# Sixteen experts on one core: the next expert's up product is issued ahead of this one's down product, into a second accumulator bank

## The reference, cut to what matters

```python
def _moe(h, w_router, b_router, w1, w3, w2):
    ...
    out = jnp.zeros_like(h)
    for e in range(N_EXPERTS):
        he = jax.nn.silu(h @ w1[e]) * (h @ w3[e])
        out = out + gates[:, e:e + 1] * (he @ w2[e])
    return out
```

## Time and profile before

| what | value |
|---|---|
| median of 3 runs | 994.59 us (994.1 to 994.79) |
| profiled execution, its own time | 996.42 us |
| profiled execution, span of the core's instructions | 994.6 us |
| PE busy | 936.2 us, 94% of the span |
| DMA | 230.74 MB, mean 232 GB/s |
| granted TensorE clock, mean | 0.986 of full |
| `up(1)` starts / `down(15)` ends | 322.9 us / 598.9 us |

### The profile page before, as it was taken

The page is one execution under the profiler, slowest core; times in us unless marked ns, Lnnn a source line. Parts: engine busy times, 40 slices in busy tenths (PEclk is TensorE's granted clock), DMA queues, the critical chain, the costliest instruction groups (busy, mean ns, idle before and its releaser), DMA issues.

```text
span 994.6 us, 11764 instructions
## 1 busy us (share of the span) xinstructions
PE 936.2 (94%) x4268; PEld 513.5 (52%) x4269; DVE 416.4 (42%) x894; ACT 304.7 (31%) x693; POOL 31.4 (3%) x54
## 2 busy tenths in 40 slices
PE   3999999999998999987999999999989999999998
PEld 1464456565443344332455445455765546577763
DVE  1279597634461012421222322601956633336452
ACT  3200534232412213340322331312465632125420
POOL 0100200000000000000000002000000000000000
PEclk9999999999999999997999999999989999999999
DMA  9998614488559799898799999404227724423401
GB/s 350 362 386 316 141 58 173 161 318 320 204 222 337 239 360 387 299 392 318 278 396 393 397 378 307 154 31 159 87 86 252 224 74 169 169 88 111 130 13 42
DMA packets 105693, 230.74 MB, mean 232 GB/s; under 512 B 3125, under 2 KB 6505, under 8 KB 105497
## 3 DMA queue, kind: packets, MB, share of 16 engines
q1 hardware_dynamic: 100288, 217.85, 61.8%
q0 software_dynamic: 2208, 7.37, 2.6%
q10 hardware_dynamic: 3128, 4.62, 1.4%
HBM read 224.31 MB, written 5.51 MB: 231 GB/s over the span
## 4 chain that ended last, share of the span: by engine, by line
PE 78%; DVE 8%; DMA 6%; ACT 4%; issue 2%; SPq 1%; POOLq 1%; ACTq 0%; POOL 0%; DVEq 0%
PE bank L646 23%; PE bank L913 12%; PE bank L926 6%; PE bank L660 5%; DMA arena<-in_w_mod_dram 5%; PE bank L943 4%; PE bank L1221 3%; PE bank L1150 3%; PE bank L1240 2%; PE bank L1231 2%; PE bank L612 2%; DMA arena<-in_gla_w_in_dram 1%; PE bank L842 1%; PE bank L938 1%; PE bank L775 1%
## 5 line engine op out<-in xcount | busy, mean ns | idle before, releaser
L646 PE MATMUL bank<-arena 128*128 128x512 f32 (+3 forms) x592 | 238.0, 560 | 4.3 <-DMA arena<-in_gla_w_in_dram 2.3
L646 PEld LDWEIGHTS bank<-arena 128*128 128x128 f32 x592 | 111.8, 191 | 122.5 <-issue 110.4
L913 PE MATMUL bank<-arena 128*64 128x512 f32 x512 | 114.6, 600 | 2.9 <-issue 2.9
L660 PE MATMUL bank<-arena 128*128 128x256 f32 (+1 forms) x384 | 99.1, 416 | 2.8 <-ACT arena L1945 1.5
L660 PEld LDWEIGHTS bank<-arena 128*128 128x128 f32 x384 | 72.1, 190 | 30.6 <-issue 21.4
L913 PEld LDWEIGHTS bank<-arena 128*64 128x64 f32 x512 | 39.4, 139 | 74.5 <-issue 73.8
L926 PE MATMUL bank<-arena,con 128*64 128x512 f32 x272 | 67.7, 644 | 4.7 <-ACT con L1848 4.0
L2395 DVE TENSOR_TENSOR con<-con,bank 128x256 f32<-128x256 f32 x17 | 7.1, 420 | 111.1 <-ACT con L1753 111.1
L1749 ACT ACTIVATE con<-bank 128x256 f32<-128x256 f32 x17 | 6.5, 384 | 139.9 <-PE bank L913 139.9
L926 PEld LDWEIGHTS bank<-arena,con 128*64 128x64 f32 x272 | 22.3, 147 | 39.7 <-issue 38.6
L612 PE MATMUL bank<-arena,silu_c 128*32 128x512 f32 x272 | 35.9, 652 | 5.6 <-DMA arena<-in_w_mod_dram 4.1
(11 more groups left out here) (415 smaller groups left out, 1207.1 us busy)
## 6 DMA issues: line engine op xcount, KB each, us to landing
arena<-in_w_gate_e_dram SPq DMA_DIRECT2D x16, 2048.0 KB, 14.5
arena<-in_w_up_e_dram SPq DMA_DIRECT2D x16, 2048.0 KB, 13.2
arena<-in_w_down_e_dram SPq DMA_DIRECT2D x16, 2048.0 KB, 12.8
arena<-in_w_mod_dram SPq DMA_DIRECT2D x12, 2048.0 KB, 16.4
arena<-in_mod_w_dram SPq DMA_DIRECT2D x12, 2048.0 KB, 8.2
arena<-in_ab_w_in_dram SPq DMA_DIRECT2D x7, 2048.0 KB, 9.2
arena<-in_gla_w_in_dram SPq DMA_DIRECT2D x6, 2048.0 KB, 16.2
arena<-in_cd_w_in_dram SPq DMA_DIRECT2D x6, 2048.0 KB, 7.8
```

The costliest lines, as they stand in the source:

```text
L646: mm = pe.matmul(ps[:, 0:n], lhs[:, k, tile * P:(tile + 1) * P], w[:, k, c0:c0 + n], start=(k == 0), stop=(k == kd_ - 1))
L660: mm = pe.matmul(ps[:, i * n:(i + 1) * n], w[:, k, c * P:(c + 1) * P], rhs[:, k, 0:n], start=(k == 0), stop=(k == KC - 1))
L913: mm = pe.matmul(up_b[64 * j:64 * j + 64, :], h[:, k, :], blocks[:, g + n:u + n + 1:u - g, :], start=(k == 0), stop=(k == KC - 1), tile_po ...
```

## The change

TensorE's order of work is written anew for experts 1 to 15. `up(e + 1)` now stands ahead of `behind_up(e)`, that is ahead of the context work, the turning and the down product of expert e. It writes a second bank, `moe3`, taken from the rotating ones after expert 0; even experts use the first, odd ones the second. The surplus rounds of expert e + 1 stand behind `down(e)` and behind what context work follows it. SyncE's rule for a slot with gate or up weights of expert e now asks for `x_up` past that expert's surplus rounds as well, for every expert: `x_up` counts three per expert, whether the rounds run or not, and TensorE adds them where the surplus rounds stand. The slot table, the order of loads, and the programs of ScalarE, VectorE and GpSimd stay, but for the bank that they read.

```diff
             moe = [banks.open(pe, f"moe{i}", experts_done, 1) for i in range(3)]
-            up_b, t_b, dn_b = moe
+            up_b, t_b, dn_b = [moe[0]], moe[1], moe[2]
             banks.hold([f"moe{i}" for i in range(3)])
 
-            def up(h, e, sem_, gathered=False):
+            def up(dst, h, e, sem_, gathered=False):
                 g, u = (slot_at(s) // 256 for s in expert_slot[e][0:2])
...
-                        mm = pe.matmul(up_b[64 * j:64 * j + 64, :], h[:, k, :], blocks[:, g + n:u + n + 1:u - g, :],
+                        mm = pe.matmul(dst[64 * j:64 * j + 64, :], h[:, k, :], blocks[:, g + n:u + n + 1:u - g, :],
                                        start=(k == 0), stop=(k == KC - 1), tile_position=(0, 64 * j))
...
@@ -959,7 +962,7 @@
                     flag = pe.value_load(flags[:, bass.ds(n, 1)], min_val=0, max_val=1)
                     with pe.If(flag > 0):
                         pe.wait_ge(x_h, n + 1)
-                        up(hs_x, e, x_up)
+                        up(up_b[surplus_bank(e)], hs_x, e, x_up)
                         pe.wait_ge(x_ff, n + 1)
                         turn_ff(x_turned)
                         landed_expert(e, 2)
@@ -1092,35 +1095,49 @@
                 pe.wait_ge(ffT_ready, e + 1)
                 down(e, down_done)
 
-            for e in range(NE):
+            def up_of(e):
                 for j in range(2):
                     landed_expert(e, j)
-                if e == 0:
-                    up(hg[:, :, 0:CAP], e, up_done, True)
+                pe.wait_ge(hs_ready, e)
+                up(up_b[e % 2], hs[e % 2], e, up_done)
+
+            def extras_of(e):
                 any_extra = pe.value_load(flags[:, e * EXTRA:e * EXTRA + 1], min_val=0, max_val=1)
-                if e == 0:
-                    with pe.If(any_extra > 0):
-                        ctx_latents(6)
-                        gather()
-                        behind_up(e)
-                        extras(e)
-                    with pe.Else():
-                        no_extras()
-                        c_place[0] -= 6
-                        ctx_latents(6)
-                        gather(True)
-                        behind_up(e)
-                    pe.wait_ge(x_down, EXTRA)
-                    continue
                 with pe.If(any_extra > 0):
                     extras(e)
                 with pe.Else():
                     no_extras()
-                pe.wait_ge(hs_ready, e)
-                up(hs[e % 2], e, up_done)
+
+            for j in range(2):
+                landed_expert(0, j)
+            up(up_b[0], hg[:, :, 0:CAP], 0, up_done, True)
+            any_extra = pe.value_load(flags[:, 0:1], min_val=0, max_val=1)
+            with pe.If(any_extra > 0):
+                ctx_latents(6)
+                gather()
+                behind_up(0)
+                extras(0)
+            with pe.Else():
+                no_extras()
+                c_place[0] -= 6
+                ctx_latents(6)
+                gather(True)
+                behind_up(0)
+            pe.wait_ge(x_down, EXTRA)
+            up_b.append(banks.open(pe, "moe3", experts_done, 1))
+            banks.hold([f"moe{i}" for i in range(4)])
+            for j in range(2):
+                landed_expert(1, j)
+            extras_of(1)
+            up_of(1)
+            for e in range(1, NE):
+                if e + 1 < NE:
+                    up_of(e + 1)
                 behind_up(e)
                 ctx_work(CTX_WORK_BEHIND.get(e, []))
-            for i in range(3):
+                if e + 1 < NE:
+                    extras_of(e + 1)
+            for i in range(4):
                 banks.filled(f"moe{i}", pe.drain())
             banks.give_back()
 
@@ -1398,8 +1415,10 @@
                     if s == 3 and e0 == 0:
                         banks.wait(sp, "qkT311")
                     sp.wait_ge(down_done if j0 == 2 else up_done, e0 + 1)
-                    if e0 == 0:
-                        sp.wait_ge(x_down if j0 == 2 else x_up, EXTRA + (0 if j0 == 2 else 1))
+                    if j0 < 2:
+                        sp.wait_ge(x_up, EXTRA * (e0 + 1) + 1)
+                    elif e0 == 0:
+                        sp.wait_ge(x_down, EXTRA)
...
-            def sigmoid(step, at):
-                act.activation(act1, up_b[:, 0:256], ACT.Exp, scale=-1.0).then_inc(step, 1)
+            def sigmoid(src, step, at):
+                act.activation(act1, src[:, 0:256], ACT.Exp, scale=-1.0).then_inc(step, 1)
...
                 act.wait_ge(up_done, e + 1)
-                sigmoid(sig_step, 2 * e).then_inc(silu_done, 1)
+                sigmoid(up_b[e % 2], sig_step, 2 * e).then_inc(silu_done, 1)
                 slot0 = slot_of(act, e * (1 + EXTRA))
...
-            def gated(sem_, value, step, at):
+            def gated(src, sem_, value, step, at):
                 dve.wait_ge(sem_, value)
-                dve.tensor_tensor(act1, act1, up_b[:, 0:256], ALU.mult).then_inc(step, 1)
+                dve.tensor_tensor(act1, act1, src[:, 0:256], ALU.mult).then_inc(step, 1)
                 dve.wait_ge(step, at + 1)
-                return dve.tensor_tensor(act2, act1, up_b[:, 256:512], ALU.mult)
+                return dve.tensor_tensor(act2, act1, src[:, 256:512], ALU.mult)
...
+        def surplus_bank(e):
+            return (e + 1) % 2 if e else 0
+
```

More of the change, by code:

```diff
@@ L1797, in behind_store @@
                     latent_T(1)
-            up_b, t_b, dn_b = [banks.banks[banks.at[f"moe{i}"][0]] for i in range(3)]
+            up_b, (t_b,), (dn_b,) = ([banks.banks[banks.at[f"moe{i}"][0]] for i in at] for at in ((0, 3), (1,), (2,)))
             def store(buf, row0, sem_):
@@ L1815, in extras @@
                             act.wait_ge(x_up, n + 2)
-                            sigmoid(x_sig_step, n * 2).then_inc(x_silu, 1)
+                            sigmoid(up_b[surplus_bank(e)], x_sig_step, n * 2).then_inc(x_silu, 1)
                             act.wait_ge(x_turned, n + 1)
@@ L2531, in extras @@
                             dve.wait_ge(x_up, n + 2)
-                            gated(x_silu, n + 1, x_gated, n).then_inc(x_ff, 1)
+                            gated(up_b[surplus_bank(e)], x_silu, n + 1, x_gated, n).then_inc(x_ff, 1)
                             dve.wait_ge(x_down, n + 1)
@@ L2551, in _ @@
                 dve.wait_ge(up_done, e + 1)
-                gated(silu_done, e + 1, up_gated, e).then_inc(ff_ready, 1)
+                gated(up_b[e % 2], silu_done, e + 1, up_gated, e).then_inc(ff_ready, 1)
                 behind_ff(e)
```

## The result

| | before | after |
|---|---|---|
| median | 994.69 us (994.1 to 996.32, 4 runs) | 1083.9 us (1078.81 to 1086.54, 4 runs) |
| profiled execution, its own time | 996.42 us | 1086.52 us |
| span | 994.6 us | 1084.7 us |
| granted TensorE clock, mean | 0.986 | 0.953 |
| `up(1)` starts / `down(15)` ends | 322.9 / 598.9 us | 321.1 / 690.6 us |

The changed kernel takes 1.0896 times as long (95% interval 1.0849 to 1.0943). Forecast were 1076 us and a range of 1053 to 1097.

What follows compares the result with a forecast made beforehand. TensorE, busy for 94% of the span, was taken to bound the kernel. Load waits 65.6 + last expert 2.3 - gain 5.6 + slow clock 18.7 = 81.0 us more, giving a median of 1076 us, range 1053 to 1097.

Steps and rivals of the forecast that it cites:

- its own case: Whole kernel: the forecast of 1076 us with a clock cost between 1.0 and 2.4 us a wait; chance 0.55.
- The loads: Experts' stage: `up` waits for weights loaded into slots freed too late, ten waits, 65.6 us in sum.
- The gain ahead of `turn_ff`: Experts 5 to 9: `up(e + 1)` covers the late activations, so waits of 3.9 us go.
- The last expert: Expert 15: no `up` is left to cover its activations, so `turn_ff(15)` waits 3.7 us instead of 1.43, 2.3 more.
- The clock: Behind each of eleven long waits TensorE runs slowly: 1.7 us each, 18.7 in all, bounds per wait 0 and 3.4.
- the clock stayed up: Rival, behind the waits: same waits but no slow clock, 62.3 us more, 1057 us; chance 0.13.
- cost double: Rival, behind the waits: the slow clock costs 3.4 us per wait, 99.7 us more, 1094 us; chance 0.17.
- Loads did not share evenly: Rival, experts 10 to 12 chiefly: loads share the rate, each landing after 20.2 us, 1146 us in all; chance 0.05.
- the weights could be there in time: Rival, experts' stage: slots come free early enough, leaving a gain of 3.3 us, 991.3 us; chance 0.04.
- The prediction's ground: Experts 7, 8, 10, 11 and 12: `down` reads the slot the next `up` needs, which no timing moves.
- Its sign: Trace after: idle time ahead of `up` put down to a DMA into arena at ten experts, near 8.4 us at five.
- nothing happens: Rival, whole kernel: the new order hides 3.9 us and loses as much, 995 us; chance 0.03.

Runs made afterwards that it cites:

- tiny_stores: Changed kernel with each experts' store cut from 64 rows to one and the buffer filled early by three other stores; 1086.2 us, ratio 1.0958 to the kernel before.
- n_after: Changed kernel without the weight loads of experts 3 to 15 and expert 2's gate and up loads; 988.38 us, ratio 0.9964 to the kernel before.
- fill_short: Changed kernel with 9 unread products ahead of the weight waits of experts 7, 8, 10, 11 and 12; 1076.54 us, 8.6 us less than the changed kernel rerun.
- early_free: Changed kernel without SyncE's wait for `x_up` at gate and up slots, except experts 0 and 8; 1075.67 us, 9.5 us less than the changed kernel rerun.
- new_table: Changed kernel with another slot table for the later experts, found by replay; 1071.21 us, 13.9 us less than the changed kernel rerun.
- fill_waits: Changed kernel with 16 unread products ahead of the weight waits of experts 7, 8, 10, 11 and 12; 1100.6 us, ratio 1.1087 to the kernel before.

## Why the prediction was right, and where its terms were off

The profiled execution grew by 90.1 us, forecast 81.0. Net of what went away, waits grew by 73.6 us (forecast 65.6 + 2.3 - 3.9 = 64.0) and busy time by 20.0 (forecast 18.7 - 1.7 = 17.0); 3.5 us fell outside the stage. The median grew by less, 89.2 us, since the profiled execution is among the longer of its four. The mechanism and the places were right; the sum is 9 us short, and 1083.9 lies just outside the 1068 to 1083 that the prediction gave its own case. That it is no more than 9 is in part luck, since misses of both signs stand in it. By the prediction's own steps:

- **The loads: 65.6 forecast, 74.4 measured**, at experts 4, 5, 6, 7, 8, 10, 11, 12, 13, 14 and 15: 6.18, 3.47, 6.18, 10.09, 9.00, 9.98, 9.45, 9.50, 4.31, 1.90 and 4.36 us. Ten of these were forecast, and experts 2, 3 and 9 wait for no load, as forecast; expert 14's 1.90 was taken for nothing. The term that was mis-sized is the duration of a load, 8.4 by the earlier trace rows and 9.3 to 10.8 in fact at 7, 8, 10, 11 and 12: +7.9 at these five. At 7 part of it is that the load stood behind another one, issued at 437.26 and landed at 446.6; why the others took longer is open (`tiny_stores`). Expert 4 waited 2.5 more, its load taking 10.5 us behind others. Expert 6 waited 2.2 less, for the reason below, and expert 15 1.6 less.
- **The gain ahead of `turn_ff`: 3.9**, as forecast; no such wait is left at experts 5 to 9. `n_after` shows that the last expert takes most of it back. The slow stretch behind expert 5's wait went too, as forecast: `down(5)` takes 3.65 us at 433.57, and took 5.35 at 407.40 before.
- **The last expert: 2.3 forecast**, 2.14 + 2.75 - 1.43 = 3.5 measured. The wait is split between a context product and `turn_ff`. ScalarE does come to its activations behind the stores, as forecast. The 2.14 us were not in the working: the context product needs a multiplication of VectorE (L2500), and that stands behind the one after `down(14)`.
- **The clock: 1.7 per wait forecast, 2.1 measured**, which is what the ten `up` products behind the waits of 3.4 us and more took above 7.05 us, 21.0 us together; `down(15)` and the product ahead of it add 2.6. The wait of 1.90 us left `up(14)` at 7.09, and the window over the wait shows 1.00. So the cost lies between the bounds of 0 and 3.4, near the value taken. The rule of the Trainium skill (TensorE: Matmul & The Clock Gate, HAM oscillation), a slow clock behind every single wait for a DMA, holds for ten of the eleven waits here; `fill_short` took 8.6 us back without shortening any load.
- **The rivals.** Behind the waits for loads the clock stayed up nowhere but at expert 14, and it never cost double (2.9 us at the most, at expert 5). Loads did not share evenly: those awaited at 7 to 12 took 10.8 us at the most, not 20.2. That the weights could be there in time falls with `early_free`. The prediction's ground, that at 7, 8, 10, 11 and 12 `down` reads the very slot that the next `up` needs, is right for four of the five; at 7 it is the context product behind `down(5)`, as its own list of the loads has it. Its sign that TensorE's idle time would be put down to a DMA came at only four of the eleven waits, and the times of the loads had to stand in for it. And that nothing happens holds only without loads (`n_after`).

## What to carry to other kernels

Before a product is moved ahead to hide a wait of an engine, count what its old place was hiding: here a round of 14 us lay over a load, and moving `up` by one place gave 4 us of waits for 74. Where buffers are all in use, the time to follow is from the last read of a buffer to the first read of what replaces it; if no work is left between the two, the whole load is paid, and the clock behind it. A lookahead asks for free buffers of its own first; that it would pay with them no run here shows, and the trial without its loads puts what it could be worth at 1 us. Look also at the last step of such a chain, or at any where the old order comes back: there nothing covers the work that was hidden.

## What the runs showed of the hardware beyond that

- A semaphore that TensorE raises in its own queue, without a product, can run ahead of products that stand in front of it. The weights of expert 6 were issued at 414.31 us, while the `down(4)` that stands ahead of the count ran from 413.20 to 416.85. Loads that wait for the end of a product came only after it (525.05 in `new_table`, where `down(8)` runs from 521.40 to 525.00).
- An fp32 product of 128x512 takes 0.87 to 0.89 us at full clock and shows as two matmuls (L1100, x18 and 7.99 us for nine in `fill_short`, x32 and 13.90 us for sixteen in `fill_waits`).
- The time of a 2 MB load is 8.3 us in the earlier trace rows, and 8.2 to 10.8 us for those that TensorE waits for at experts 4 to 13 here; the spread is not explained in full.
- Idle times of 2 to 3 us ahead of `up` went either way with the clock: `up` took 7.09 us behind 2.27 us (`early_free`, expert 15) and 2.93 us (`after`, expert 9), and 8.54 behind 2.48 us (`early_free`, expert 14) and 8.71 behind 2.60 us (the kernel before, expert 8).
- The kernel before itself moves between 987.64 and 996.07 us from run to run on one chip (25 runs), which is 0.8%, and more than the change gains where it gains anything.
